# The low parts of all weight tiles: from VectorE to a program on GpSimd

## The chip, the cores and the metric

The kernel runs on one core of one Trainium2 chip. The core has TensorE (matrix products into PSUM), VectorE and ScalarE (elementwise work), GpSimd (elementwise work on SBUF only) and SyncE, which here only issues transfers. They run side by side and meet at semaphores. The metric is the device time of one execution in microseconds; lower is better.

## The reference, cut to what matters

The input is one sequence of 1024 positions with 1024 features, in float32. It goes through three blocks, in short:

```
# first block
proj = rmsnorm(x, mix_norm_g) @ w_in                      # q, k, v, g, u, sv
ret = silu(g) * rmsnorm(retention_chunkwise(rotary(q), rotary(k), v))
sgu = spatial_gating_chunked(gelu(u), gelu(sv))
x = x + concatenate([ret, sgu]) @ w_out
a, b = split(causal_depthwise_conv(rmsnorm(x, ffn_norm_g) @ w_up))   # width 3
x = rmsnorm(x + (silu(a) * b) @ w_down, final_norm_g)                # 2816 wide
# second block
glu_a, glu_b, z_conv, q, k, v, z_att = split(rms_norm(x) @ w_in + b_in)
y_conv = conformer_conv(glu_a, glu_b)         # glu_a * sigmoid(glu_b), 31 taps,
                                              # layer norm, silu, @ pw_w
y_att = neighbourhood_attention(q, k, v, rpb) # 8x16 windows of a 16x64 grid
y = concatenate([grouped_rms_norm(y_conv) * silu(z_conv),
                 grouped_rms_norm(y_att) * silu(z_att)])
x = rms_norm(x + y @ w_out, final_g)
# third block
h = layer_norm(x)
mix = concatenate([rms_norm(stick_breaking_attention(q, k, v)),
                   rms_norm(sliding_window_attention(q, k, v))]) @ w_out   # from h @ w_in
h = layer_norm(ALPHA * h + mix)
gate, up = split(h @ w_gate_up)
return layer_norm(ALPHA * h + (silu(gate) * up) @ w_down)            # 2816 wide
```

Each block has norms over the features before and after its parts. Nearly all of the arithmetic is in the products `h @ w` of the activations with the weight matrices, and these have to be as exact as a float32 product.

## The kernel before, in words

The activations lie transposed, with features on the 128 partitions and the 1024 positions along the row. The residual `x` stays in SBUF for the whole kernel.

**Weight stream.** All weights are packed into one stream of 228 tiles of 128x1024 float32 (512 KB each). A tile is what one output of 128 features needs from all 1024 inputs, or a part of an MLP down projection, or half of the pointwise product. For a product that is close to float32, each weight is split into two float32r numbers: w_hi, a rounded copy, and w_lo = w_raw - w_hi. The activations are split in the same way into h_hi and h_lo. Each product is then three matmuls, `w_hi h_hi + w_lo h_hi + w_hi h_lo`, in `gemm` (line 407) or, where two tiles run together behind a norm, in `project_pair` (line 437). A tile is 48 matmuls of 128x512.

**Who does what for tile t.** Each of w_raw, w_hi and w_lo has two buffers, used by tiles of even and odd number.
- SyncE loads w_raw (line 2109) once w_lo of tile t-2 has been made.
- ScalarE copies w_raw into w_hi (line 866) once the load has landed and TensorE is through with tile t-2.
- VectorE subtracts (line 1436) once w_hi of tile t is there.
- TensorE takes tile t once w_lo of tile t is there.

**Order.** Each engine's program is one Python class that writes its instructions in the order in which the engine runs them; there is no planner. `split_up_to(t)` in `ScalarProgram` and in `VectorProgram` puts the splits of all tiles up to t, as far as they haven't been issued, at the place of the call. So on both engines a split stands in a queue with the norms, taps, softmax steps and residual sums around it, and what is behind a split waits for what the split waits for. `Queue.wait_ge` leaves out a wait that the engine has passed before.

**Places that come up below.**
- A pair of tiles follows each norm or each mixer: tiles 0, 24, 32, 98, 128, 136, 154 and 162 and the ones after them.
- First MLP (tiles 32 to 97): per group of six tiles, up projections `a` and `b` with three taps each on ScalarE and VectorE, their product `mlp_tp`, its parts `mlp_act_hi` and `mlp_act_lo` (line 1686), and two down tiles whose eight sums VectorE adds to the residual (line 1680). At its end, VectorE also sums squares (line 1600).
- Conformer (tiles 98 to 109): for each of four channel tiles VectorE forms conv_u (line 1721) and runs 24 taps (28 for the last) over it, alternately into y and conv_part (line 1734); TensorE runs the other taps (line 628) and then a mean over the four tiles (line 448).
- `y_low` (line 1457 through `low`), `rotary` (lines 1511 to 1515), the last steps of neighbourhood attention (lines 1834 and 1838), and the sum for the layer norm's mean (line 2040).
- GpSimd has one instruction of the program, a memset (line 2150) whose result SyncE waits for at the start.

## Time and profile before

| | |
|---|---|
| time, median of 3 runs | 3603.32 us (3598.68 to 3607.8) |
| the profiled execution | 3605.6 us, of which the span from first to last instruction is 3604.3 us |
| mean granted TensorE clock in it | 0.969 |
| TensorE busy | 3386.6 us, 94% |
| VectorE busy | 1570.9 us, 44% |
| ScalarE busy | 1121.3 us, 31% |
| GpSimd busy | 0.4 us |

Busy time is the time in which an engine has an instruction in flight, as a share of the span. A matmul's end is modelled, and matmuls overlap, so one of 400 ns starts every 234 ns. An idle time is put down to the instruction whose semaphore came last.

### The profile page before, as it was taken

Reading aid. Unit: us, or ns where it says so; the run is one execution under the profiler, and the core shown is the slowest. Engines: PE = TensorE matmul, PEld = TensorE weight load, DVE = VectorE, ACT = ScalarE, POOL = GpSimd, SP = SyncE. Lnnn points to the kernel's source line nnn. Section 1 sums busy time; section 2 is a strip of 40 time slices with the busy share of each in tenths; the row PEclk is TensorE's granted clock in tenths of the full one; section 3 lists DMA queues with packets and bytes.
Section 4 is the critical chain, followed back from the end, with each engine's and each line's share of the span. In section 5 each row is a group of like instructions: output and inputs, shape, how many; then the busy total and the mean of one; then the engine's idle time right before and its main releaser. Section 6 shows DMA issues by size and latency. Waiting matters only on the chain. (4 is left out here: it accounts for less than half of the span.)

```text
span 3604.3 us, 33001 instructions
## 1 busy us (share of the span) xinstructions
PE 3386.6 (94%) x13906; PEld 2495.8 (69%) x13906; DVE 1570.9 (44%) x2227; ACT 1121.3 (31%) x1603; POOL 0.4 (0%) x5
## 2 busy tenths in 40 slices
PE   8999899999999899899999899999869999999997
PEld 5887678888888667566667545546347688888885
DVE  4432354444445589433334532342573432332334
ACT  3223332222122331544442532342561411111113
POOL 0000000000000000000000000000000000000000
PEclk9999999999999999999999999998999999999998
DMA  3211111111111101101001000000001111111111
GB/s 128 75 54 38 32 40 48 52 41 53 47 47 47 41 28 31 35 24 30 24 24 41 30 12 24 18 6 18 7 18 41 30 53 47 47 47 47 47 47 53
DMA packets 48818, 141.76 MB, mean 39 GB/s; under 512 B 12790, under 2 KB 16670, under 8 KB 48542
## 3 DMA queue, kind: packets, MB, share of 16 engines
q1 hardware_dynamic: 48670, 139.65, 12.7%
q8 instruction: 110, 1.80, 0.2%
q14 instruction: 38, 0.31, 0.0%
HBM read 135.36 MB, written 9.77 MB: 40 GB/s over the span
## 5 line engine op out<-in xcount | busy, mean ns | idle before, releaser
L407 PE MATMUL psum<-h_hi,w_hi 128*128 128x512 f32 x2656 | 846.9, 400 | 9.9 <-DVE w_lo L1436 3.1
L407 PE MATMUL psum<-h_lo,w_hi 128*128 128x512 f32 x2656 | 838.5, 397 | 0.0
L407 PE MATMUL psum<-h_hi,w_lo 128*128 128x512 f32 x2656 | 838.5, 397 | 0.0
L407 PEld LDWEIGHTS psum<-h_hi,w_hi 128*128 128x128 f32 x2656 | 499.0, 189 | 141.8 <-issue 19.9
L407 PEld LDWEIGHTS psum<-h_lo,w_hi 128*128 128x128 f32 x2656 | 501.1, 189 | 122.0
L407 PEld LDWEIGHTS psum<-h_hi,w_lo 128*128 128x128 f32 x2656 | 500.9, 189 | 122.2
L1436 DVE TENSOR_TENSOR w_lo<-w_raw,w_hi 128x1024 fp32r<-128x1024 f32 x228 | 278.6, 1222 | 619.1 <-ACT w_hi L866 619.0
L866 ACT ACTIVATE w_hi<-w_raw 128x1024 fp32r<-128x1024 f32 x228 | 239.4, 1050 | 457.5 <-PE psum L407 386.8
L1680 DVE TENSOR_TENSOR residual<-residual,psum 128x1024 f32<-128x1024 f32 x176 | 214.6, 1219 | 170.4 <-PE psum L407 169.3
L407 PE MATMUL psum<-mlp_act_hi,w_hi 128*128 128x512 f32 x704 | 219.8, 394 | 12.8 <-DVE mlp_act_lo L1686 11.3
L407 PE MATMUL psum<-mlp_act_hi,w_lo 128*128 128x512 f32 x704 | 218.6, 392 | 0.0
L407 PE MATMUL psum<-mlp_act_lo,w_hi 128*128 128x512 f32 x704 | 218.5, 392 | 0.0
L407 PEld LDWEIGHTS psum<-mlp_act_hi,w_hi 128*128 128x128 f32 x704 | 133.5, 190 | 42.3 <-DVE mlp_act_lo L1686 12.2
L407 PEld LDWEIGHTS psum<-mlp_act_hi,w_lo 128*128 128x128 f32 x704 | 133.5, 190 | 28.2
L407 PEld LDWEIGHTS psum<-mlp_act_lo,w_hi 128*128 128x128 f32 x704 | 133.3, 189 | 27.9
L1079 ACT ACTIVATE mlp_act_hi<-mlp_tp 128x1024 fp32r<-128x1024 f32 x44 | 46.6, 1060 | 321.5 <-DVE mlp_tp L2058 233.1
L1629 DVE SCALAR_TENSOR_TENSOR mlp_tb<-psum,vectors,mlp_tb 128x1023 f32<-128x1023 f32 (+1 forms) x44 | 56.4, 1282 | 162.8 <-ACT mlp_tb L1019 162.0
L437 PE MATMUL psum<-h_hi,w_hi 128*128 128x512 f32 x256 | 88.0, 427 | 34.7 <-ACT h_hi L919 15.3
L1892 DVE TENSOR_SCALAR sb_mag<-psum 128x512 f32<-128x512 f32 (+3 forms) x96 | 52.9, 557 | 147.1 <-PE psum L754 147.0
L2058 DVE TENSOR_TENSOR mlp_tp<-mlp_ta,psum 128x1024 f32<-128x1024 f32 x22 | 26.9, 1221 | 180.1 <-PE psum L407 178.3
L763 PE MATMUL psum<-sb_soft,common 128*128 128x512 f32 (+3 forms) x192 | 98.1, 597 | 5.3 <-DVE sb_soft L1908 5.3
L754 PE MATMUL psum<-sb_q,sb_k 64*128 64x512 f32 (+3 forms) x192 | 94.7, 602 | 4.9 <-ACT sb_vtok L1294 4.9
(272 smaller groups left out, 3419.1 us busy)
## 6 DMA issues: line engine op xcount, KB each, us to landing
w_raw<-in_weights SPq DMA_DIRECT2D x228, 512.0 KB, 3.6
residual<-in_x_t SPq DMA_DIRECT2D x8, 512.0 KB, 8.6
out_t<-residual SPq DMA_DIRECT2D x8, 512.0 KB, 3.0
rel_copies<-rel_rows SPq DMA_DIRECT2D x8, 480.0 KB, 6.3
na_bias<-rel_copies SPq DMA_DIRECT2D x8, 240.0 KB, 4.2
band_copies<-band_rows SPq DMA_DIRECT2D x8, 192.0 KB, 6.2
ret_rotary<-in_rotary SPq DMA_DIRECT2D x1, 1024.0 KB, 8.2
swa_bias<-band_copies SPq DMA_DIRECT2D x4, 256.0 KB, 2.7
```

The costliest lines, as they stand in the source:

```text
L407: ins = self.pe.matmul(out[:, s], w[:, k, at:at + P], src(k, low)[:, s], start=(k == 0 and part == 0), stop=(k == n_k - 1 and part == 2))
L437: ins = pe.matmul(out[j][:, s], w[:, k, :], self.h(k, low)[:, s], start=(k == 0 and part == 0), stop=(k == KD - 1 and part == 2))
L754: pe.matmul(z[:, c0:HALF], m.sk[hp, kb * CH:(kb + 1) * CH], m.sq[hp, qh * HALF + c0:(qh + 1) * HALF], start=True, stop=False, skip_group_c ...
L763: ins = pe.matmul(z[:, c0:HALF], m.c("neg_tri"), m.soft[:, i % 3, c0:HALF], start=False, stop=False, skip_group_check=True)
L866: self.act.activation(self.m.w_hi[:, n % 2, :], self.m.raw[:, n % 2, :], ACT.Copy).then_inc(*self.to("w_hi", n))
L1079: self.act.activation(m.act_hi[:, c % 2, :], m.tp[:], ACT.Copy).then_inc(*self.to("act_hid_hi" + name, c))
L1436: self.dve.tensor_tensor(self.m.w_lo[:, n % 2, :], self.m.raw[:, n % 2, :], self.m.w_hi[:, n % 2, :].bitcast(F32), ALU.subtract).then_inc( ...
L1629: dve.scalar_tensor_tensor(y[:, back:S], m.place["proj", t][:, 0:S - back], w, y[:, back:S], ALU.mult, ALU.add).then_inc(*to("dve_tap_" + ...
L1680: self.dve.tensor_tensor(x, x, self.m.place["down", t, n], ALU.add).then_inc(*self.to("dve_down", t, n))
L1892: dve.tensor_scalar(m.mag[:, i % 4, c], m.place["pe_sz", p, i][:, c], LN_TOP, None, ALU.min).then_inc(*to("dve_slow", p, i))
L2058: dve.tensor_tensor(m.tp[:], m.ta[:], m.place["proj", b[c]], ALU.mult).then_inc(*to("dve_mmlp3", c))
```

## The change

All calls of `VectorProgram.split_up_to` go, and with them the method. A new program for GpSimd holds the subtractions of all 228 tiles in a row, each behind its wait for w_hi. It begins with the memset that stood in the code of SyncE's program. In the MLP of the third block the wait for `mlp_act_hi` of the product before becomes a wait for its `mlp_act_lo`.

```diff
-    def split_up_to(self, t):
-
-        while self.next_split <= min(t, N_TILES - 1):
-            n = self.next_split
-            self.q.wait_ge(*self.on("w_hi", n))
-            self.dve.tensor_tensor(self.m.w_lo[:, n % 2, :], self.m.raw[:, n % 2, :], self.m.w_hi[:, n % 2, :].bitcast(F32),
-                                   ALU.subtract).then_inc(*self.to("w_lo", n))
-            self.next_split += 1
...
         for i in range(CONV_TILES - 1):
             t = B2 + 2 + 2 * i
-            self.split_up_to(t + 1)
             taps(i, 0, TAPS // 4)
-            self.split_up_to(t + 2)
             taps(i, TAPS // 4, TAPS - PE_TAPS)
             total(i, TAPS - PE_TAPS)
             gated(i + 1)
...
             q.wait_ge(*on("proj", b[c]))
             if c:
-                q.wait_ge(*on("act_hid_himlp3", c - 1))
+                self.after("dve_hid_lomlp3", c - 1)
             dve.tensor_tensor(m.tp[:], m.ta[:], m.place["proj", b[c]], ALU.mult).then_inc(*to("dve_mmlp3", c))
...
+class PoolProgram:
+
+
+    def __init__(self, nc, mem, s):
+        self.q, self.pool, self.m, self.on, self.to = Queue(nc.gpsimd), nc.gpsimd, mem, s.on, s.to
+
+    def program(self):
+        m = self.m
+        self.pool.memset(m.y[0:NA_HEADS * REL_H, KD - 1, 0:REL_PAD], 0.0).then_inc(*self.to("pool_padded"))
+        for n in range(N_TILES):
+            self.q.wait_ge(*self.on("w_hi", n))
+            self.pool.tensor_tensor(m.w_lo[:, n % 2, :], m.raw[:, n % 2, :], m.w_hi[:, n % 2, :].bitcast(F32),
+                                    ALU.subtract).then_inc(*self.to("w_lo", n))
...
-        self.nc.gpsimd.memset(padded, 0.0).then_inc(*self.to("pool_padded"))
         q.wait_ge(*on("pool_padded"))
...
         VectorProgram(nc, mem, s).program()
+        PoolProgram(nc, mem, s).program()
         SyncProgram(nc, mem, s, tensors).program()
```

## Rows read from the trace of the kernel before

**Rows 1.** the page, busy time, share and instructions of each engine.
```profile
PE 3386.6 (94%) x13906; PEld 2495.8 (69%) x13906; DVE 1570.9 (44%) x2227; ACT 1121.3 (31%) x1603; POOL 0.4 (0%) x5
```

**Rows 2.** the page, costliest groups: xcount | busy us, mean ns | idle before.
```profile
L1436 DVE TENSOR_TENSOR w_lo<-w_raw,w_hi 128x1024 fp32r<-128x1024 f32 x228 | 278.6, 1222 | 619.1 <-ACT w_hi L866 619.0
```

**Rows 3.** TensorE's waits: us in total, times, longest.
```profile
PE psum L437 <- DVE w_lo L1436: 9.4, 2, 5.7
```

**Rows 4.** timeline (start us, us), tile 26, behind a pair.
```profile
417.48 1.06 ACT L866 ACTIVATE w_hi<-w_raw 128x1024 fp32r<-128x1024 f32 x1 [14.83 <-PE psum L437]
421.44 0.63 PE L407 MATMUL psum<-h_hi,w_hi 128*128 128x512 f32 x2
```

**Rows 5.** timeline, first MLP, tile 41.
```profile
598.05 1.04 ACT L866 ACTIVATE w_hi<-w_raw 128x1024 fp32r<-128x1024 f32 x1
598.18 1.22 DVE L1686 TENSOR_TENSOR mlp_act_lo<-mlp_tp,mlp_act_hi 128x1024 fp32r<-128x1024 f32 x1 [1.13 <-ACT mlp_act_hi L1079]
602.93 0.63 PE L407 MATMUL psum<-h_hi,w_hi 128*128 128x512 f32 x2
```

**Rows 6.** groups of instructions on GpSimd.
```profile
L2150 POOL MEMSET y<- 120x128 f32 x1 | 0.2, 205 | 0.3 <-POOLq L2310 0.3
L2310 POOL MEMSET const-float32-0.0<- 128x1 f32 x1 | 0.1, 100 | 0.2 <-issue 0.2
```

**Rows 7.** timeline, tile 113.
```profile
1518.64 1.06 ACT L866 ACTIVATE w_hi<-w_raw 128x1024 fp32r<-128x1024 f32 x1 [4.82 <-DVE na_q L1806]
1521.08 0.74 PE L407 MATMUL psum<-h_hi,w_hi 128*128 128x512 f32 x2 [3.11 <-DVE w_lo L1436]
```

**Rows 8.** timeline, start of the kernel.
```profile
24.30 2.36 DVE L1436 TENSOR_TENSOR w_lo<-w_raw,w_hi 128x1024 fp32r<-128x1024 f32 x2 [24.30 <-ACT w_hi L866]
27.80 0.75 DVE L1451 SCALAR_TENSOR_TENSOR norm_buf<-residual,vectors,norm_rstd 128x512 f32<-128x512 f32 x1 [1.15 <-ACT norm_rstd L877]
58.49 0.70 PE L407 MATMUL psum<-h_hi,w_hi 128*128 128x512 f32 x2 [1.34 <-DVE ret_q L1513]
```

**Rows 9.** conformer: stretch, length, busy PE PEld DVE ACT POOL, clock, DMA; then timeline.
```profile
1305.00:1339.00 34.00, 34.00 (x123) 23.00 (x122) 33.90 (x30) 6.17 (x11) 0.00 (x0) 1.00 0.11 31
1338.27 1.22 DVE L1721 TENSOR_TENSOR conv_u<-conv_ga,conv_gb 128x1024 f32<-128x1024 f32 x1
1371.89 1.22 DVE L1721 TENSOR_TENSOR conv_u<-conv_ga,conv_gb 128x1024 f32<-128x1024 f32 x1
1445.33 1.22 DVE L1743 TENSOR_TENSOR y<-y,psum 128x1024 f32<-128x1024 f32 x1
1339.54 0.70 PE L628 MATMUL psum<-conv_u,conv_diags 128*128 128x512 f32 x1
1374.15 0.59 PE L628 MATMUL psum<-conv_u,conv_diags 128*128 128x512 f32 x1
1449.91 7.03 PE L448 MATMUL psum<-y,common 128*128 128x512 f32 x16
```

**Rows 10.** timeline, end of the first MLP, tile 98.
```profile
1237.00 1.04 ACT L866 ACTIVATE w_hi<-w_raw 128x1024 fp32r<-128x1024 f32 x1
1238.27 2.35 DVE L1600 TENSOR_TENSOR norm_acc<-norm_acc,norm_buf 128x1024 f32<-128x1024 f32 x2
1240.54 1.22 DVE L1436 TENSOR_TENSOR w_lo<-w_raw,w_hi 128x1024 fp32r<-128x1024 f32 x1
1254.33 3.75 PE L614 MATMUL psum<-norm_acc,common 128*128 128x512 f32 x4 [4.97 <-DVE norm_acc L1600]
```

**Rows 11.** timeline, before the second mixer's output, tile 129.
```profile
1895.90 1.04 ACT L866 ACTIVATE w_hi<-w_raw 128x1024 fp32r<-128x1024 f32 x1
1897.34 1.23 DVE L1838 TENSOR_TENSOR y<-na_t,na_gate 128x1024 f32<-128x1024 f32 x1
```

**Rows 12.** timeline, before the third block's second layer norm, tile 163.
```profile
2795.37 1.06 ACT L866 ACTIVATE w_hi<-w_raw 128x1024 fp32r<-128x1024 f32 x1 [10.18 <-PE psum L407]
2796.57 1.23 DVE L2040 TENSOR_TENSOR norm_acc<-norm_acc,residual 128x1024 f32<-128x1024 f32 x1
```

More of the change, by code:

```diff
@@ L1462, in program @@
         m = self.m
-        self.split_up_to(1)
         self.split_norm("n1", (m.n_buf0, m.n_buf1), m.n_rstd, lambda k: m.v("mix_norm_g", k), "act_n1_rstd")
@@ L1495, in y_low @@
     def y_low(self, block, ahead):
-        self.split_up_to(ahead)
         for k in range(KD):
@@ L1519, in retention @@
         mask, qdec, cdec = m.table[:, 0:P], m.table[:, P:2 * P], m.table[:, 2 * P + 1:2 * P + 2]
-        self.split_up_to(2)
         q.wait_ge(*on("rotary_loaded"))
@@ L1553, in retention @@
                 ins.then_inc(*(to("dve_rchain", h, n) if n < NCH - 1 else to("dve_rstate", h)))
-            self.split_up_to(t + 3)
             if h < RET_HEADS - 1:
@@ L1558, in retention @@
             dve.tensor_scalar(m.y[:, h, :], m.place["pe_ro", h], m.v("ret_norm_g", h), None, ALU.mult).then_inc(*to("dve_ro", h))
-            self.split_up_to(t + 4)
             if h < RET_HEADS - 1:
@@ L1576, in gating @@
             dve.tensor_tensor(m.rk[:], m.rk[:], m.place["pe_smean", g], ALU.subtract).then_inc(*to("dve_scent", g))
-            if g < SGU_GROUPS - 1:
-                self.split_up_to(t + 1)
             q.wait_ge(*on("act_srstd", g, 1))
@@ L1583, in gating @@
             dve.tensor_tensor(w_t, w_t, m.c("tril_t"), ALU.mult).then_inc(*to("dve_swm", g))
-            if g < SGU_GROUPS - 1:
-                self.split_up_to(t + 2)
             q.wait_ge(*on("pe_smix", g))
@@ L1642, in up @@
             self.hidden("mlp1", c)
-        self.split_up_to(MLP1 + 2)
         taps_a(0)
         up(0)
-        self.split_up_to(MLP1 + 3)
         taps_a(1)
-        self.split_up_to(MLP1 + 4)
         up(1)
@@ L1652, in mlp1 @@
             c = 2 * g
-            self.split_up_to(a[c] + 1)
             for half in range(2):
                 t = d[2 * g - 2 + half]
-                self.split_up_to(t + 1)
                 for n in range(4):
@@ L1660, in mlp1 @@
                         tap(m.ta, "a", a[c], c, c, 1 + n)
-            self.split_up_to(b[c] + 1)
             up(c)
-            self.split_up_to(a[c + 1] + 1)
             taps_a(c + 1)
-            self.split_up_to(b[c + 1] + 1)
             up(c + 1)
@@ L1668, in mlp1 @@
             t = d[2 * NGROUP - 2 + half]
-            self.split_up_to(t + 1)
             for n in range(4):
@@ L1707, in norm4 @@
         dve.tensor_tensor(m.gains[:], m.vec[:, g3:g3 + KD], m.vec[:, g4:g4 + KD], ALU.mult).then_inc(*to("dve_gains"))
-        self.split_up_to(B2 + 1)
         self.combine("n4", "act_n3_rstd", ("pe_n4_mean",))
@@ L1746, in conformer @@
         dve.memset(m.u[:, PAD + S:], 0.0)
-        self.split_up_to(B2 + 2)
         gated(0)
@@ L1753, in conformer @@
             t = B2 + 2 + 2 * i
-            self.split_up_to(t + 1)
             taps(i, 0, TAPS // 4)
-            self.split_up_to(t + 2)
             taps(i, TAPS // 4, TAPS - PE_TAPS)
@@ L1761, in conformer @@
         for j in range(CONV_TILES):
-            self.split_up_to(B2 + 8 + j + 1)
             taps(i, 9 * j, min(9 * j + 9, n))
@@ L1794, in pointwise @@
         for n in range(4):
-            if n % 2 == 0:
-                self.split_up_to(B2 + 13 + n // 2)
             if n:
@@ L1809, in neighbourhood @@
             t = B2 + 14 + 4 * p
-            self.split_up_to(t + 1)
-            self.split_up_to(t + 2)
             q.wait_ge(*on("na_bias_loaded", p))
@@ L1814, in neighbourhood @@
                               ALU.add).then_inc(*to("dve_nmask", p))
-            self.split_up_to(t + 3)
-            self.split_up_to(t + 4)
             self.after("dve_nmask", p)
@@ L1855, in after_mix2 @@
             ins.then_inc(*to("dve_l1_acc", n))
-        self.split_up_to(B3 + 1)
         q.wait_ge(*on("pe_l1_mean", 1))
@@ L1880, in stick_breaking @@
         dve, q, m, on, to = self.dve, self.q, self.m, self.on, self.to
-        self.split_up_to(B3 + 2)
         dve.tensor_copy(m.ident_b[:], m.c("ident"))
@@ L1884, in stick_breaking @@
         for p in range(4):
-            self.split_up_to(B3 + 2 + 4 * p + 4)
             q.wait_ge(*on("pe_svtok", p))
@@ L1946, in add_squares @@
             dve.tensor_tensor(m.total[:, s], m.total[:, s], m.y[:, p, s], ALU.add).then_inc(*to("dve_wtotal", p, half))
-        self.split_up_to(B3 + 19)
         q.wait_ge(*on("sinks_loaded"))
@@ L2077, in mlp3 @@
             t = d[2 * NGROUP - 2 + half]
-            self.split_up_to(t + 1)
             for n in range(4):
```

18 lines of the change are left out of this document (removed).

## The prediction, written before the changed kernel was run

> **What bounds the kernel now.** I read the page's totals first: TensorE is busy for 3386.6 us of the 3604.3 us span, VectorE for 1570.9, GpSimd for 0.4 [rows 1]. The table of costliest groups then says where VectorE's time goes: the moved instruction, line 1436, is its largest group, 228 times 1222 ns, 278.6 us [rows 2]. It would be easy to call that a gain of 278 us. So the third view is TensorE's list of waits, and there w_lo stands with 9.4 us in two waits on line 437 and one 3.1 us wait on line 407 [rows 3, 7]. The rest of TensorE's idle time (3604.3 - 3386.6 = 218 us in all) belongs to norms, softmax loops and activation chains. The weight split is a side stream: the kernel ends when TensorE has gone through its 228 tiles, and VectorE matters only where TensorE waits for it.
>
> **What must stay true for the stream to be hidden.** ScalarE makes w_hi of tile t once tile t-2 is finished, then w_lo follows, and tile t starts when TensorE has done tile t-1. I compared the end of w_hi with the first matmul for all tiles. Three kinds matter.
> - Most tiles have 5 to 12 us there.
> - In the first MLP two tiles of each group of six have less. Tile 41: w_hi ends at 598.05 + 1.04 = 599.09, its first matmul starts at 602.93, so 3.84 us; VectorE is in a product with two SBUF inputs until 599.40, which leaves 3.53 us behind that [rows 5]. There are 20 such tiles, and tile 35, with 3.3.
> - The tile behind a pair (26, 100, 130, 156, 164) has 421.44 - 418.54 = 2.90 us [rows 4].
> - Tile 113 has none to spare: w_hi ends at 1519.70 and TensorE starts at 1521.08 after a 3.11 us wait; the 1.38 us between them are the subtraction and its hand-overs [rows 7].
>
> **What one subtraction costs on GpSimd (D).** The trace has no such instruction. The only rows are memsets: 120x128 in 205 ns, 128x1 in 100 ns [rows 6]. The slope is 105 / 127 = 0.83 ns a column. A subtraction has two streams in and one out. If all three overlapped, D = 0.10 + 1024 x 0.83 ns = 0.95 us, the lower end. If each cost a whole memset, eight times the 205 ns row, D = 3 x 1.64 = 4.9 us, the upper end. One after another at the slope: 0.10 + 3 x 0.85 = 2.6 us. I take 2.4, near that, since some overlap is likely. The Trainium skill, "GPSIMD Engine Reference", section 3.1, gives 4497 ns for a float32 tensor_tensor of 2048 columns; half is 2.25 us, an estimate of mine from that page, and by it the sum below would be about 1 us smaller.
>
> **The changes, part by part, without contention between the two engines.**
> - 228 subtractions leave VectorE. Hidden by TensorE everywhere but at these places. Tile 2's stands ahead of the first rotary; TensorE waits 1.34 us for that rotary at 58.49 [rows 8], and the 1.23 us go: -1.2. Tile 98's, at 1240.54, stands in a stretch where VectorE is back to back up to the norm sum that TensorE awaits for 4.97 us [rows 10]: -1.1. Tile 129's holds up TensorE by its last 0.1 us only: h_hi, made from the y product that ends at 1898.57, takes another 1.1 us [rows 11], and is needed too: -0.1.
> - The conformer is where VectorE is full: 33.90 busy of 34.00 us [rows 9]. It is not the bound there: TensorE is busy 34.00 of 34.00. Its taps of channel tile 1 start at 1339.54, 0.05 us behind the conv_u product (1338.27 + 1.22), so the subtractions taken off VectorE there, ten of 1.13 us (what one adds back to back: two such instructions last 2.35 us [rows 10]), buy 0.1.
> - 228 subtractions come to GpSimd, which does nothing else: 228 x 2.4 = 547 us in a span of 3604. Tile 113: D replaces 1.22, TensorE starts +1.2 later. Tiles behind pairs: 2.4 < 2.90, hidden. MLP tiles: hidden. The cover ends at D = 2.9 for five tiles and at 3.8 for 21.
> - The padded memset is issued from the new program as its first instruction, as now: 0. In the last MLP, product c now waits for VectorE's own low part c-1, which ended many us before, while line 2058 waits for a projection anyway: 0. No DMA is added or moved; a load waits for w_lo of two tiles before, and has around 11 us over its 3.6.
> Sum: -1.2 - 1.1 - 0.1 - 0.1 + 1.2 = -1.3 us.
>
> **With contention.** Every VectorE instruction at these places that I use below has two SBUF inputs, as has the subtraction on GpSimd; today all of that runs on one engine, so no row shows them side by side. The bound from below is no interference (the sum above). From above: GpSimd keeps VectorE out for the whole of D. I take the upper end, as a mechanism of this kernel: both engines pull two float32 streams from the same partitions at the same moment. The Trainium skill, "SBUF — State Buffer", section "Who interferes with whom", states just this rule: a VectorE instruction with two SBUF inputs and a GpSimd one that reads SBUF exclude each other, and the second waits in full. No row here shows it; by it the sum is the one that follows, without it the one above.
> - Conformer. Taps are scalar_tensor_tensor with conv_u and an accumulator, back to back. Up to conv_u of channel tile 1, three subtractions (tiles 101 to 103) would hold VectorE for 3 x 2.4 = 7.2 while two of 1.13 are gone: +4.9. The next round has two of each: +4.8 - 2.3 = +2.5, sum 7.4; but that conv_u ends at 1373.11 and TensorE's taps start at 1374.15, 1.04 of slack [rows 9]. TensorE: +6.4. The end adds nothing: VectorE would be 10 x (2.4 - 1.13) = 12.7 late, from 1446.55 to 1459.3, and the last four of the sixteen mean matmuls, 5.2 us into the row of 1449.91, would be at 1461.5.
> - Tile 98: w_hi is done at 1238.04, norm_acc starts 1238.27 [rows 10]. GpSimd is first, VectorE loses 2.4 and has saved 1.13: +1.2 in place of -1.1.
> - Tile 129: w_hi done 1896.94; either the y product of 1897.34 goes first and w_lo ends at 1901.0 (+1.2), or GpSimd does and y is 2.4 late [rows 11]. Taken: +1.8.
> - Tile 163: w_hi done 2796.43, norm_acc on the way to the layer norm's mean starts 2796.57 [rows 12]: 0 or +2.4, taken +1.2.
> - Start: the subtractions of tiles 0 and 1 would last from 24.3 to 29.1; the first scaling at 27.80 slips [rows 8]: by 1.3, of which some 0.5 falls into the wait that its second half has anyway: +0.8.
> - Unchanged: tile 2 -1.2, tile 113 +1.2.
> Sum: 6.4 + 1.2 + 1.8 + 1.2 + 0.8 - 1.2 + 1.2 = +11.4 us. The profiled execution took 3605.6 (span 3604.3 and 1.3 around it), 2.3 above the median of 3603.3; so 3617.0 in its terms, and 3614.7 for the median. I give **3614 us**.
>
> **Rivals.**
> - No contention: the first sum, 3603.3 - 1.3 = **3602**. For it: nothing in the trace shows interference, all of it is assumed. This is the case on the other side, faster than before, by tile 98 and the rotary; it decides if VectorE's taps take what they take now beside a GpSimd instruction. Even then it is far less than 0.3%. To reach 0.3% TensorE would have to lose 11 us of waits of which w_lo and what stands behind it hold at most 12.5 + 2.4.
> - GpSimd is slow, D = 4.9: w_lo becomes late on its own. 21 tiles x (4.9 - 3.6) = 27, five pairs x 2.0 = 10, tile 113 3.7, and in the conformer (3 x 4.9 - 2.3) + (9.8 - 2.3) - 1.0 = 19 with contention. About +45 without, +65 with it: **3650 to 3670**. Against it: it needs twice my D; float32r output is the one thing that the memset rows can't speak for.
> - VectorE keeps GpSimd out: back-to-back taps leave no opening until the one-SBUF-input sum with psum at the end of each channel tile. That is at about 1337, while two tiles of 11.5 us stand before the taps of 1339.54, so the first of them is due at 1316: TensorE would stand some 20 us in each of three rounds, **3660**. Against: a waiting instruction would have to be passed over some twenty times.
> - The subtraction isn't moved at all (a low part still on VectorE): the diff takes out every call, so I give it nothing.
>
> **How the numbers follow.** Contention at about D = 2.4: 0.55. Its own range, D from 2.0 to 3.0 and with half to all of D lost, is 3607 to 3622. No contention: 0.28. Slow GpSimd: 0.09. VectorE keeping GpSimd out: 0.08. The range 3600 to 3635 leaves out the centres of the last two, 0.17 of the chance, and little else. A measurement of this kernel tells about 0.3% (11 us, so 3592.5 and 3614.1) from no change. The likeliest case lies at that border: half of it is slower, half the same. Slower: 0.27 + 0.09 + 0.08 = 0.44. Same: 0.28 + 0.25 = 0.53. Faster: 0.03.
>
> **What would show it.** In the profile after: about 228 GpSimd subtractions with D read off directly; VectorE's total down by 279 us if nothing interferes, but its tap rows longer than now, or gaps between them, if it does. TensorE's list of waits should have conv_u at 1340 and 1375 with some 5 us and 1.5 us, and no rotary at 58. The time from w_hi to the first matmul of tile 113 gives D plus the hand-over. I am wrong in the mechanism if the taps are untouched, and wrong in size if D is over 3 us or if w_lo turns up in TensorE's waits in the MLPs.

## The result, and the profile after

| | before | after |
|---|---|---|
| time, us: median (lowest to highest), runs beside each other | 3604.2 (3598.7 to 3607.8), 4 | 3635.9 (3628.9 to 3641.5), 4 |
| ratio, 95% interval | 1 | 1.0092 (1.0078 to 1.0105) |
| profiled execution, time and span | 3605.6, 3604.3 | 3641.5, 3640.1 |
| VectorE busy | 1570.9 | 1374.3 |
| TensorE busy, mean granted clock | 3386.6, 0.969 | 3402.8, 0.962 |

The kernel is 31.6 us slower by the medians. My forecast was 3614 and my range ended at 3635.

The group of the moved instruction in the changed kernel's page, and TensorE's waits (us in total, times, longest):

```profile
L2043 POOL TENSOR_TENSOR w_lo<-w_raw,w_hi 128x1024 fp32r<-128x1024 f32 x228 | 589.8, 2587 | 2986.5 <-ACT w_hi L866 2986.5
```
```profile
PE psum L437 <- ACT h_hi L927: 11.4, 2, 7.7
PE psum L407 <- POOL w_lo L2043: 15.6, 2, 11.4
PE psum L628 <- DVE conv_u L1686: 5.0, 1, 5.0
PE psum L454 <- DVE norm_acc L1984: 4.7, 1, 4.7
PE psum L454 <- DVE norm_acc L1806: 0.8, 1, 0.8
```

Three things are to be seen. VectorE lost 228 instructions that took 278.6 us [rows 2], but only 196.6 us of busy time: 82 us came back, in instructions that last longer than before. The mean of a subtraction on GpSimd is 2587 ns, and 198 of the 228 last less than 2.5 us (the shortest 2.34); two last 9.7 and 27.0 and lift the mean. And w_lo still stands in TensorE's waits: not with the 9.4 us of [rows 3], but with one wait of 11.4 us that was not there.

That wait is in the conformer. The timeline of the changed kernel there, GpSimd first, then VectorE, then TensorE (start us, us):

```profile
1330.52 9.67 POOL L2043 TENSOR_TENSOR w_lo<-w_raw,w_hi 128x1024 fp32r<-128x1024 f32 x1 [21.48 <-ACT w_hi L866]
1340.82 2.66 POOL L2043 TENSOR_TENSOR w_lo<-w_raw,w_hi 128x1024 fp32r<-128x1024 f32 x1 [0.63 <-ACT w_hi L866]
...
1419.31 30.33 POOL L2043 TENSOR_TENSOR w_lo<-w_raw,w_hi 128x1024 fp32r<-128x1024 f32 x2 [8.88 <-ACT w_hi L866]
```
```profile
1336.67 1.28 DVE L1699 SCALAR_TENSOR_TENSOR conv_part<-conv_u,vectors,conv_part 128x1024 f32<-128x1024 f32 x1
1337.98 3.29 DVE L1705 TENSOR_TENSOR y<-y,conv_part 128x1024 f32<-128x1024 f32 x1
...
1342.44 2.12 DVE L1686 TENSOR_TENSOR conv_u<-conv_ga,conv_gb 128x1024 f32<-128x1024 f32 x1
...
1442.84 1.28 DVE L1699 SCALAR_TENSOR_TENSOR conv_part<-conv_u,vectors,conv_part 128x1024 f32<-128x1024 f32 x1
1444.15 3.25 DVE L1705 TENSOR_TENSOR y<-y,conv_part 128x1024 f32<-128x1024 f32 x1
```
```profile
1344.61 2.07 PE L628 MATMUL psum<-conv_u,conv_diags 128*128 128x512 f32 x2 [5.03 <-DVE conv_u L1686]
...
1446.37 1.22 PE L407 MATMUL psum<-h_hi,w_hi 128*128 128x512 f32 x2 [11.36 <-POOL w_lo L2043]
```

The subtraction of tile 103 starts at 1330.52, and the taps of VectorE go on at 1.28 us each, untouched. Only the sum at 1337.98, which comes 0.03 us behind the end of the last tap because it waits for that tap's own result, is 3.29 us long in place of 1.22, and 2.2 us into it GpSimd is done. So GpSimd did nothing for 7.5 us and then all its work behind the first opening. Tile 108 (the first of the two in the 30.33 us row, up to 1446.32) is the same over 20 boundaries between taps: asked at 1419.31, through at 1444.15, and TensorE had wanted the tile since 1435.0.

The second thing is TensorE's clock. "Granted clock" is the share of full speed: 1.00 is 2.4 GHz, 0.50 is 1.2 GHz, and a value between them means that the stretch holds both. Stretches of the changed kernel behind these waits and behind two layer norms (length, busy PE PEld DVE ACT POOL, granted clock, DMA):

```profile
1342.00:1352.00 10.00, 7.39 (x12) 3.31 (x13) 9.96 (x10) 1.11 (x1) 1.48 (x1) 0.66 0.27 89
1446.00:1456.00 10.00, 9.63 (x31) 7.70 (x32) 2.62 (x2) 0.00 (x0) 3.64 (x2) 0.71 0.36 107
2022.00:2035.00 13.00, 9.69 (x12) 3.36 (x11) 9.12 (x8) 5.50 (x7) 0.71 (x1) 0.50 0.13 40
2827.00:2841.00 14.00, 9.05 (x11) 3.38 (x12) 10.13 (x8) 3.17 (x3) 1.32 (x1) 0.51 0.12 37
```

In the kernel before, the same four places had 1.00, 1.00, 0.87 and 0.88. At the second layer norm of the third block TensorE waits 4.71 us for a sum in place of 2.57, and is granted 1.2 GHz for 13.7 us in a row where the kernel before had 3.4 us of it. How much of this comes from the longer wait is taken up behind experiment 12.

To place the whole loss I took the time from the first matmul of one tile to that of another, in every trace (us; the last line is after minus before):

```
tiles         0-2   98-100  100-103 103-107 107-110 110-116 116-130 130-136 136-154 154-164 164-227
before       27.5    23.9    57.7    64.5    57.9   133.3   317.4    99.3   681.1   141.0   707.8
after        24.9    25.2    65.0    64.5    70.2   135.4   320.4   103.7   681.4   147.0   706.4
difference   -2.6    +1.4    +7.3     0.0   +12.4    +2.1    +3.0    +4.3    +0.2    +6.0    -1.4
```

With +1.0 at the start, +0.4 in tiles 2 to 97 and +1.7 behind tile 227 these are the 35.8 us between the two spans. 19.7 of them are in the conformer (tiles 100 to 110), some 15 at four places where a norm or a product is due (tiles 113, 129, 137, 163).

### The profile page after: what moved, and what is told of

Its sections match the earlier page's. It is cut to its first block and busy times, and to the rows that moved or that the text cites. A ratio compares the mean times of both kernels' runs of the same rounds, so it can differ in the third digit from the quotient of the medians.

```text
span 3640.1 us, 33002 instructions
## 1 busy us (share of the span) xinstructions
PE 3402.8 (93%) x13906; PEld 2504.8 (69%) x13906; DVE 1374.3 (38%) x1999; ACT 1121.5 (31%) x1603; POOL 590.2 (16%) x233
## 5 line engine op out<-in xcount | busy, mean ns | idle before, releaser
L2043 POOL TENSOR_TENSOR w_lo<-w_raw,w_hi 128x1024 fp32r<-128x1024 f32 x228 | 589.8, 2587 | 2986.5 <-ACT w_hi L866 2986.5
```

Of the source, the lines that this page charges most:

```text
L2043: self.pool.tensor_tensor(m.w_lo[:, n % 2, :], m.raw[:, n % 2, :], m.w_hi[:, n % 2, :].bitcast(F32), ALU.subtract).then_inc(*self.to("w_lo ...
```

## The experiments

Each kernel ran beside the kernel before on its chip, whose medians there were 3600.3 to 3600.8 us. All kernels that split the subtractions between the two engines have this in VectorE's loop, and the set ON_POOL differs:

```diff
+            self.next_split += 1
+            if n in ON_POOL:
+                continue
             self.q.wait_ge(*self.on("w_hi", n))
```

**1. The conformer's ten subtractions back on VectorE.**
```diff
+ON_POOL = set(range(N_TILES)) - set(range(101, 111))
```


> The changed kernel with the ten subtractions of tiles 101 to 110 (conformer) back on VectorE at their old places, all others on GpSimd. Theory (VectorE's back-to-back two-input taps and GpSimd exclude each other, and in the conformer GpSimd can be kept out until VectorE itself waits): TensorE gets back the 5.0 us wait on conv_u, the 11.4 us wait on w_lo of tile 108 and the slow clock behind both; by the difference of the two traces, tile by tile, 7.3 + 11.5 + 2.6 - 1.7 = 19.7 us less than the changed kernel: about 3616, 12 above the kernel before. Rival (GpSimd slows VectorE a little everywhere, and the conformer has no special part; then ten subtractions of 228 carry 4% of the loss): 3634 to 3636.

Measured: 3620.1 us (3618.2 to 3624.7), ratio 1.0051 (1.0034 to 1.0068), so 19 above the kernel before. By the trace the conformer's part is gone, to the last tenth: tiles 100 to 110 take 178.4 us, where before has 180.1 and after 199.8. The rival falls. I had put too little outside the conformer: the other places hold more than 12 us (15 by the traces, 19 by the medians).

**2. Only these ten on GpSimd.**
```diff
+ON_POOL = set(range(101, 111))
```


> The kernel before with only the subtractions of tiles 101 to 110 on GpSimd. Theory: it loses in the conformer what the changed kernel lost there, 5.0 us at conv_u of channel tile 1, 11.4 at tile 108 if GpSimd is locked out again, and the slow clock behind: 3604 + 20 = 3624; if a lock-out is a matter of which moment GpSimd asks in, single executions scatter between +8 (no lock-out) and +20 or more. Rival (loss spread over all tiles): 3604 to 3607.

Measured: 3629.5 us, ratio 1.0082 (1.0052 to 1.0112); the four executions took 3622.2, 3626.4, 3632.6 and 3640.9. By the medians ten instructions of 228 bring most of the loss (ratio 1.0082 of 1.0092), and with them the executions scatter over 19 us. But this ratio and that of experiment 1 (1.0051) add up to more than the whole, so it overstates the ten's share: in the profiled execution tiles 100 to 110 take 193.4 us, 13.3 more than before, and the rest of the 20.4 us between the two spans lies where nothing was changed (3.6 at tiles 154 to 164, 2.9 at 138 to 154, and smaller ones). In the one profiled (3626.4) GpSimd's rows are:

```profile
1330.38 9.70 POOL L2113 TENSOR_TENSOR w_lo<-w_raw,w_hi 128x1024 fp32r<-128x1024 f32 x1 [21.46 <-ACT w_hi L871]
...
1436.27 17.60 POOL L2113 TENSOR_TENSOR w_lo<-w_raw,w_hi 128x1024 fp32r<-128x1024 f32 x2 [15.32 <-ACT w_hi L871]
```

Tile 103 is kept out for 9.7 us as in the changed kernel; tile 108 gets in at once this time (2.57 us), and tile 109 is kept out for 14.3 (the first of the two in the second row).

**3. VectorE stops for GpSimd.**
```diff
+            self.after("w_lo", t + 1)
             taps(i, 0, TAPS // 4)
+            self.after("w_lo", t + 2)
             taps(i, TAPS // 4, TAPS - PE_TAPS)
...
+            self.after("w_lo", B2 + 8 + j + 1)
             taps(i, 9 * j, min(9 * j + 9, n))
```


> The changed kernel, but VectorE waits for GpSimd's low part at the places in the conformer where it used to make that low part itself (before tap 0 and 7 of channel tiles 0 to 2, before taps 0, 9, 18, 27 of the last). Nothing is moved back; VectorE only stops there until GpSimd is done. Theory (GpSimd is kept out by VectorE's unbroken row of taps): no GpSimd subtraction of 10 or 27 us is left, tile 108 has its low part before it is due, the 11.4 us wait and the slow clock behind it go: 12 to 14 us less than the changed kernel, about 3622 to 3624; the 5 us wait on conv_u stays. Rival (tile 108 was late because GpSimd is slow beside taps, not because it was kept out; then an additional wait of VectorE can only cost): 3636 or more, and single subtractions of over 5 us stay.

Measured: 3623.6 us (3623.2 to 3627.9), ratio 1.0061 (1.0045 to 1.0078) against 1.0092 for the changed kernel: ten waits more, 11 us less. GpSimd and VectorE around tile 108:

```profile
1418.88 4.50 POOL L2046 TENSOR_TENSOR w_lo<-w_raw,w_hi 128x1024 fp32r<-128x1024 f32 x1 [8.73 <-ACT w_hi L866]
```
```profile
1419.90 1.28 DVE L1699 SCALAR_TENSOR_TENSOR y<-conv_u,vectors,y 128x1024 f32<-128x1024 f32 x1
1423.42 1.29 DVE L1699 SCALAR_TENSOR_TENSOR conv_part<-conv_u,vectors,conv_part 128x1024 f32<-128x1024 f32 x1 [2.24 <-POOL w_lo L2046]
```

The subtraction was passed over at one boundary (1419.90), VectorE stopped at 1421.18, and 2.2 us after that it was done. Tiles 107 to 110 take 56.2 us (70.2 in the changed kernel); the 7.3 us at tile 103 stay, as expected. A stop of VectorE lets a waiting GpSimd in. That the subtraction would have stayed out for the rest of the row without it is seen in the changed kernel, not in this run. I had also written that no long subtraction would be left; tile 103's is (9.7 us), since its stop comes later than its lock-out.

**4. Taps with one SBUF input.** The accumulation of taps 2 and up is left out.
```diff
-                    ins = dve.scalar_tensor_tensor(out, src, w, out, ALU.mult, ALU.add)
+                    ins = dve.tensor_reduce(out[:, 0:1], src, AX_X, ALU.add)
```


> The changed kernel, in which taps 2 and up of the conformer on VectorE are sums over the row (tensor_reduce: one SBUF input, one column out) in place of scalar_tensor_tensor with two SBUF inputs; it leaves out the accumulation of the depthwise convolution. VectorE stays back to back in them, each reading 1024 columns. Theory (two SBUF inputs are what collides with GpSimd): no GpSimd subtraction that starts within these reductions lasts more than 2.6 us, none of the reductions is put off, the waits on conv_u and on w_lo of tile 108 and the slow clock behind them are gone: about 20 us less than the changed kernel, 3612 to 3617. Rival (any unbroken row of VectorE instructions keeps GpSimd out): the 10 and 27 us subtractions stay, as does the time.

Measured: 3617.2 us, ratio 1.0044 (1.0028 to 1.0061). VectorE and GpSimd at tile 108, and VectorE at tile 104:

```profile
1410.32 1.21 DVE L1699 TENSOR_REDUCE y<-conv_u 128x1 f32<-128x1024 f32 x1
1411.45 1.21 DVE L1699 TENSOR_REDUCE conv_part<-conv_u 128x1 f32<-128x1024 f32 x1
...
1338.42 0.81 DVE L1694 TENSOR_SCALAR y<-conv_u,vectors 128x1024 f32<-128x1024 f32 x1
1339.14 2.85 DVE L1696 TENSOR_SCALAR conv_part<-conv_u,vectors 128x1024 f32<-128x1024 f32 x1
```
```profile
1410.76 2.36 POOL L2043 TENSOR_TENSOR w_lo<-w_raw,w_hi 128x1024 fp32r<-128x1024 f32 x1 [9.70 <-ACT w_hi L866]
...
1339.10 2.35 POOL L2043 TENSOR_TENSOR w_lo<-w_raw,w_hi 128x1024 fp32r<-128x1024 f32 x1 [7.89 <-ACT w_hi L866]
```

Beside the reductions neither engine sees the other, though their row is as unbroken as that of the taps. So it is not VectorE's being busy. The edit changed one thing more: a reduction writes one column and a tap 1024. That the writing is not what collides is seen in the changed kernel, in the sum behind the one that was held up at tile 108. It has one input in SBUF and one in PSUM, writes 1024 columns, and lasts 1.22 us as before although it falls into the second subtraction of the 30.33 us row above:

```profile
1447.44 1.22 DVE L1708 TENSOR_TENSOR y<-y,psum 128x1024 f32<-128x1024 f32 x1
```

The same holds for the 40 residual sums with PSUM that overlap a subtraction in that trace (1.22 us each).

One instruction with a single SBUF input does collide, the tensor_scalar at 1339.14: it takes 0.75 us for 1024 columns when alone (the reductions 1.21) and 2.85 here. A copy in the changed kernel does so too (2.82 in place of 0.69). The Trainium skill, "SBUF — State Buffer", section "Who interferes with whom", has both: a VectorE instruction contends with GpSimd's reads if it has two SBUF inputs or runs in one of the modes that use both ports, and not otherwise. The trace agrees on two inputs against one; that the tensor_scalar and the copy run in such a mode no row says, only that they are the quick ones. Tiles 100 to 110 take 178.9 us.

**5. The lock-out by itself.** All low parts on VectorE; twelve subtractions that nobody needs on GpSimd.
```diff
+        for i in range(CONV_TILES):
+            for j in (3, 8, 16):
+                q.wait_ge(*on("dve_tap", i, j))
+                if cols := next(delays):
+                    self.pool.memset(m.probe[:, 2, 0:cols], 0.0)...
+                self.pool.tensor_tensor(m.probe[:, 2, :], m.probe[:, 0, :], m.probe[:, 1, :], ALU.subtract)...
```


> The kernel before, all low parts on VectorE, with twelve subtractions of the same size that nobody needs on GpSimd beside the taps, each asked for when a certain tap has ended and delayed by 0 to 1.1 us (a memset of 0 to 960 columns in between). It measures the lock-out by itself. Theory: some of the twelve take 2.4 us and delay a tap by 2.4, others do not start until VectorE waits at the end of its channel tile, up to 20 us later, and which of the two depends on the moment within the running tap at which they ask (in the changed kernel those that asked 0.75 to 0.99 us into a tap came through, those at 0.39 and 1.03 did not); the memsets in between, with no SBUF input, last what their size says and hold up nobody. Rival (no lock-out, GpSimd always gets its turn at the next boundary between two taps): all twelve last 2.4 to 3.7 us.

The ninth and the tenth of GpSimd's pairs:

```profile
1412.68 0.80 POOL L2114 MEMSET probe<- 128x832 f32 x1 [8.38 <-DVE y L1735]
1413.56 9.64 POOL L2116 TENSOR_TENSOR probe<-probe 128x1024 f32<-128x1024 f32 x1
1431.70 0.90 POOL L2114 MEMSET probe<- 128x960 f32 x1 [8.50 <-DVE conv_part L1735]
1432.68 3.53 POOL L2116 TENSOR_TENSOR probe<-probe 128x1024 f32<-128x1024 f32 x1
```

Nine subtractions got in at the next boundary and last 2.2 us plus the rest of the tap that ran; each made the next tap 3.4 us long in place of 1.28. Two missed one boundary, one lasted 9.6 us. The memsets, which have no SBUF input, last what their size says (0.80 us for 832 columns) and delayed no tap. One of the two that missed a boundary had asked only 0.02 us ahead of it. The one of 9.6 us had asked 1.07 us into a tap, the two of 9.7 us above at 1.01 and 1.03: that looked like a window near the end of a tap.

**6. Sixteen other moments, with stops of VectorE.**
```diff
+                    if (i, j - 5) in DELAYS:
+                        self.after("pool_probed", i, j - 5)
```


> As the kernel with twelve unneeded subtractions on GpSimd beside the taps, with sixteen of them at other moments within a tap (seven at 1.0 to 1.25 us, the rest at 0.2 to 1.0, the last four of these in the last channel tile), and VectorE waits for each before the fifth tap after the one that set it off, so that no lock-out hides the next. Theory (the outcome hangs on the moment within the tap): those at 0.2 to 0.98 us get in at the next boundary and last 2.4 + the rest of the tap; those at 1.0 to 1.17 are kept out for all boundaries up to VectorE's stop, and last 5 us. Rival (it hangs on something else, as which channel tile or buffer): outcomes that differ for the same moment; the last channel tile, where one at 0.39 was kept out, is the place to look.

The theory fell. GpSimd's third and fourth, and the tap put off by the fourth:

```profile
1329.49 0.79 POOL L2116 MEMSET probe<- 128x832 f32 x1 [5.99 <-DVE y L1739]
1330.36 2.46 POOL L2118 TENSOR_TENSOR probe<-probe 128x1024 f32<-128x1024 f32 x1
1338.81 0.82 POOL L2116 MEMSET probe<- 128x864 f32 x1 [5.99 <-DVE y L1739]
1339.71 2.38 POOL L2118 TENSOR_TENSOR probe<-probe 128x1024 f32<-128x1024 f32 x1
```
```profile
1338.61 1.27 DVE L1739 SCALAR_TENSOR_TENSOR conv_part<-conv_u,vectors,conv_part 128x1024 f32<-128x1024 f32 x1
1339.81 3.37 DVE L1739 SCALAR_TENSOR_TENSOR y<-conv_u,vectors,y 128x1024 f32<-128x1024 f32 x1
```

They asked 1.07 and 1.10 us into a tap and got in at the very next boundary, as did all sixteen. The last channel tile behaved like the others.

**7. The same without the stops.** The two lines of 6 are taken out.

> The sixteen unneeded subtractions on GpSimd at the same moments, without the stops of VectorE. With the stops all sixteen came through at the first or second boundary between taps, also those at 1.03 to 1.13 us into a tap, so the moment within the tap does not decide. Theory 1 (chance: most requests come through, some are kept out, stops or not): nearly the same picture, with 0 to 4 kept out for several taps. Theory 2 (a stop a few taps ahead is what lets GpSimd in): about half of the sixteen or more are kept out until VectorE stops at the end of the channel tile.

The same sixteen durations to 0.01 us, none kept out. Theory 1's low end (0 of 16); a stop a few taps ahead is not what lets GpSimd in.

**8. Both lock-outs once more.** The changed kernel and experiment 5, unchanged.

> The changed kernel once more, for the lock-outs alone. Theory 1 (whether GpSimd gets in is fixed by the program): the subtraction of tile 103 lasts 9.7 us again and that of tile 108 27.0. Theory 2 (it changes from one execution to the next with small shifts in time; the executions of the changed kernel lay 12 us apart): tile 103, which took 9.7 us in three kernels, does so again, but 108 or 109 last something else.

> The kernel with twelve unneeded subtractions once more. Theory 1 (fixed by the program): the ninth is kept out for 9.6 us again, the tenth and the twelfth for one tap more than needed, the others for none. Theory 2 (chance from execution to execution): others are kept out, or none.

```profile
1419.54 30.32 POOL L2043 TENSOR_TENSOR w_lo<-w_raw,w_hi 128x1024 fp32r<-128x1024 f32 x2 [8.88 <-ACT w_hi L866]
```
```profile
1412.55 2.47 POOL L2116 TENSOR_TENSOR probe<-probe 128x1024 f32<-128x1024 f32 x1
...
1431.75 8.28 POOL L2116 TENSOR_TENSOR probe<-probe 128x1024 f32<-128x1024 f32 x1
```

In the changed kernel both come again to 0.02 us (9.67 and 27.00; time 3641.6). In the other kernel they don't: the ninth gets in at once, the tenth is kept out and lasts 8.3 us. It missed five boundaries and got in at the sixth, in the middle of VectorE's row, with no stop and no opening there. The tap that it put off, behind a subtraction of VectorE's own:

```profile
1436.55 1.22 DVE L1437 TENSOR_TENSOR w_lo<-w_raw,w_hi 128x1024 fp32r<-128x1024 f32 x1
1437.68 3.43 DVE L1735 SCALAR_TENSOR_TENSOR conv_part<-conv_u,vectors,conv_part 128x1024 f32<-128x1024 f32 x1
```

So neither of my theories holds alone: some places repeat, some change though the moment within the tap moved by less than 10 ns. What decides stays open, and so does whether a lock-out lasts to the end of the row. (The single executions of experiments 5 to 8 with unneeded subtractions took 3622.5 to 3630.1 us.)

**9. Two subtractions of 228.**
```diff
+ON_POOL = {137, 163}
```


> The kernel before with two of its 228 subtractions on GpSimd, those of tiles 137 and 163. They fall beside the last addition of the sums that the layer norms behind the second and third mixer wait for. Theory (each puts that addition off by 2.1 to 2.3 us; TensorE waits 0.8 and 2.1 us longer and then runs at the low granted clock): the two steps seen in all four kernels with these two on GpSimd, 4.3 and 4.3 to 5.4 us, come from them alone: 8 to 10 us more than before, about 3610. Rival (these steps have another cause and the clock drop is not tied to the two): the added waits alone, 0 to 3 us.

Measured: 3607.5 us, ratio 1.0023 (1.0014 to 1.0032): 7 to 8 us for two instructions, the low end of what I gave. The interval begins at 5 us, so they cost more than the 2.1 us that TensorE waits longer. In the profiled execution (3612.5, above the median) the step is at tile 163. VectorE, GpSimd and TensorE there, and the 14 us behind (columns as above):

```profile
2797.18 3.36 DVE L2047 TENSOR_TENSOR norm_acc<-norm_acc,residual 128x1024 f32<-128x1024 f32 x1
```
```profile
2797.11 2.34 POOL L2113 TENSOR_TENSOR w_lo<-w_raw,w_hi 128x1024 fp32r<-128x1024 f32 x1 [795.81 <-ACT w_hi L871]
```
```profile
2800.59 2.93 PE L459 MATMUL psum<-norm_acc,common 128*128 128x512 f32 x3 [4.71 <-DVE norm_acc L2047]
```
```profile
2798.00:2812.00 14.00, 8.92 (x10) 3.36 (x11) 10.13 (x8) 3.17 (x3) 1.45 (x1) 0.52 0.13 37
```

GpSimd was 0.07 us ahead, the addition took 3.36 us in place of 1.23 [rows 12], TensorE waited 2.1 us more and ran at 0.52 of its clock; tiles 154 to 162 take 5.2 us more than in the trace of before. At tile 137 VectorE's addition is held up just the same (3.37 us), but nothing comes of it: tiles 130 to 136 take 99.6 us (99.3 before). TensorE's first matmuls of the norm ran at the low clock in this execution and lasted until the second sum was there.

**10. Tiles 128 to 130 with 137.**
```diff
+ON_POOL = {128, 129, 130, 137}
```


> The kernel before with four subtractions on GpSimd, those of tiles 128, 129, 130 and 137. Tile 137's alone (with 163's) left no step behind the second mixer, while the four kernels that also had 128 to 130 on GpSimd showed 4.3 us there. Theory (the later start of the pair at tile 128, a wait of 7.7 in place of 5.7 us, comes before the wait at the norm, and the two together bring the 13.7 us at half the clock): steps of 1.5 to 2 us at tile 128 and of 4.3 us at tile 136, in all 6 us more than before. Rival (the 4.3 us need other tiles on GpSimd too): the step at 128 alone, 2 us.

Measured: 3616.4 us, ratio 1.0042 (1.0028 to 1.0056). TensorE at the layer norm, and the stretch behind it:

```profile
1998.72 2.40 PE L459 MATMUL psum<-norm_acc,common 128*128 128x512 f32 x4 [3.73 <-DVE norm_acc L1607]
2002.00 2.93 PE L459 MATMUL psum<-norm_acc,common 128*128 128x512 f32 x3 [0.88 <-DVE norm_acc L1861]
```
```profile
2000.00:2015.00 15.00, 11.57 (x16) 4.05 (x15) 11.13 (x9) 5.86 (x8) 0.87 (x1) 0.54 0.12 35
```

The steps are those of the changed kernel: tiles 116 to 130 take 320.0 us (317.4 before), 130 to 136 103.7 (99.3). In the profiled executions the 4.3 us came with the delay at tile 129 ahead of the one at 137, and not without it. The median is 16 us above before, twice the 7 us that these steps add up to; in its profiled execution tiles 138 to 154 took 654.4 us, where that stage took between 644.9 and 657.3 us over all traces whatever the kernel. I can't say how much of the 16 it holds.

**11. Lateness without GpSimd.** The computation is complete; `hold_up` is two multiplications that nobody needs.
```diff
+                if n == KD - 1:
+                    self.hold_up()
                 ins = dve.scalar_tensor_tensor(m.m_acc[:], x, g, m.m_acc[:], ALU.mult, ALU.add)
```
(and the same ahead of the last addition at the third mixer)

> The kernel before, GpSimd doing nothing, with two more VectorE multiplications of 128x1024 that nobody needs ahead of the last addition of the sums that the layer norms behind the second and the third mixer wait for. They put these two sums off by 2.3 us each, as GpSimd's subtraction did in the changed kernel. Theory (a longer wait of TensorE there costs itself plus matmuls at the low granted clock behind it, whoever causes the wait): the wait grows by 0.8 to 2.3 us in each place, TensorE is then granted 0.5 of its clock for 10 us and more, and the two places together cost 8 to 11 us, like the 4.3 and 5.2 us in the changed kernel: about +9. Rival (the slow clock has to do with GpSimd or came by chance, and a wait costs what it lasts): the sum of the longer waits alone, +3.

Measured: 3606.5 us, ratio 1.0010 (1.0000 to 1.0019), between theory and rival, and the interval (0 to 7 us) holds the rival's 3. TensorE at the third mixer, and the stretch behind it:

```profile
2794.93 2.93 PE L454 MATMUL psum<-norm_acc,common 128*128 128x512 f32 x3 [4.84 <-DVE norm_acc L2049]
```
```profile
2792.00:2806.00 14.00, 8.58 (x12) 3.22 (x13) 11.26 (x11) 3.17 (x3) 0.00 (x0) 0.63 0.14 37
```

There it looks like the theory, without GpSimd: 4.84 us of wait in place of 2.57, a clock of 0.63 in place of 0.88, and tiles 154 to 162 take 121.8 us in place of 116.9, of which 2.3 are the wait. But the trace of before is at the low end there, as the numbers behind experiment 12 show. At the second mixer the wait came out as 0.29 us and the step as 0.3, since TensorE's own first sum ran at the low clock just then (3.18 us where the changed kernel's took 2.53) and hid it.

**12. More of it at the second mixer.** Three multiplications there, none at the third.

> The kernel before with three unneeded VectorE multiplications (3.6 us) ahead of the last addition of the layer norm sum behind the second mixer, nothing at the third, and nothing on GpSimd. With two of them the sum was 2.3 us late, yet TensorE showed no wait above 0.3 us there, because its own first sum ran at the low granted clock. Theory (a wait of TensorE there brings the long low-clock stretch with it, whoever makes it): a second wait of 1 to 2 us at this layer norm, 0.5 of the clock for over 10 us as in the changed kernel, and a step of 4 to 6 us in the times of the tiles behind. Rival (the long stretch needs GpSimd): a stretch of 3.4 us as in the kernel before, and a step of 1 to 2 us, the wait itself.

Measured: 3606.6 us, ratio 1.0012 (1.0004 to 1.0021). TensorE at the second mixer:

```profile
1999.70 1.98 PE L454 MATMUL psum<-norm_acc,common 128*128 128x512 f32 x4 [1.32 <-DVE norm_acc L1861]
```
```profile
1995.00:2010.00 15.00, 11.02 (x22) 4.30 (x23) 14.06 (x13) 8.16 (x10) 0.00 (x0) 0.89 0.11 35
```

The wait is there, 1.32 us, but the clock behind it is 0.89, the short stretch of the kernel before, and tiles 130 to 136 took 100.5 us (99.3): the rival's picture, or no step at all, since five traces in which this sum was not put off have 100.8 (experiments 6, 7, 13, 14 and the repeat of 5 in 8). But the profiled execution, 3601.5 us, is the fastest of ten, and eight of the others lie at 3604.6 to 3607.5, 4 to 7 above before, which is the theory's size. The experiment does not decide; where the others lost these microseconds no trace shows.

What the steps at the two mixers are worth shows only against all traces. Ten traces have the 2.57 us wait of before at the third mixer, and tiles 154 to 162 take from 116.8 to 119.8 us in them, 118.4 in the mean; the seven with the longer wait of 4.7 or 4.8 (experiment 11's among them) take 121.5 to 122.3. So the longer wait costs some 3.6 us by the means, and of the 5.2 between the traces of before and after up to 2.9 come without it. The low clock too comes without a longer wait. Experiment 5's trace there:

```profile
2817.37 3.22 PE L455 MATMUL psum<-norm_acc,common 128*128 128x512 f32 x4 [2.57 <-DVE norm_acc L2042]
```
```profile
2818.00:2832.00 14.00, 11.51 (x19) 4.40 (x18) 9.59 (x9) 5.17 (x5) 0.00 (x0) 0.64 0.13 37
```

That is the wait of before with the clock of experiment 11. At the second mixer tiles 130 to 138 take 126.4 to 128.8 us where the sum was not put off, and 130.7 in the changed kernel. At the first channel tile of the conformer there is no such doubt: tiles 100 to 103 take 57.7 us in all eight traces in which GpSimd does nothing there, and 65.0 in the changed kernel.

**13. Everything back that stands beside a norm.**
```diff
+ON_POOL = set(range(N_TILES)) - {0, 1, 98, 99, 100, 113, 128, 129, 130, 137, 163} - set(range(101, 111))
```


> The kernel with the conformer's ten subtractions back on VectorE, and also those of tiles 0, 1, 98 to 100, 113, 128 to 130, 137 and 163, all of which stand beside a norm or a product that TensorE waits for; the 207 others on GpSimd. Theory (the loss outside the conformer sits at these few places): 3597 to 3602, no more than the kernel before, 18 to 20 us less than with the conformer's alone moved back. Rival (the softmax loops of the two attention stages, 111 to 162, lose too beside GpSimd): 5 us or more above before.

Measured: 3597.4 us, ratio 0.9994 (0.9985 to 1.0003). The 207 subtractions left on GpSimd cost nothing, their mean is 2435 ns, and 22.7 us separate this from experiment 1. TensorE's list of waits has none on GpSimd. The softmax loops did not suffer: tiles 138 to 154 took 644.9 us, the least of all traces.

**14. Only the first mixer's and the MLPs' tiles on GpSimd.**
```diff
+ON_POOL = set(range(2, 98)) | set(range(164, 228))
```


> The kernel before with the subtractions of tiles 2 to 97 and 164 to 227 on GpSimd (first mixer, both MLPs), and those of tiles 0, 1 and 98 to 163 (conformer, pointwise, neighbourhood, norms, attention blocks) on VectorE as before. Theory (the whole loss sits where TensorE waits for VectorE or w_lo): nothing is lost, and what the changed kernel gained stays: 1.3 us ahead of the first rotary and about 1.3 more in the mixer and at tile 34: 2 to 3 us less than before. Rival (GpSimd's 160 subtractions disturb VectorE everywhere, which shows in time): at least 5 us more than before.

Measured: 3597.7 us, ratio 0.9992 (0.9983 to 1.0001). Both versions lie 3 us under the kernel before, and both intervals just include no change. Of the 278.6 us [rows 2] that one hoped to take off VectorE this is what there was to gain.

## Why the prediction was wrong, by its own steps

- **D = 2.4 us: right.** The median of the 228 is 2.40 us. The page figure I had weighed ("GPSIMD Engine Reference", section 3.1, in the Trainium skill) gave 2.25 by my halving; the measurement decides.
- **Tiles behind pairs and in the MLPs hidden: right.** Tiles 164 to 227 take 706.4 us in the changed kernel and 706.3 in that of experiment 2, where VectorE makes their low parts.
- **Contention, by its upper end: right, and shown** by experiments 4 and 9. A VectorE instruction with two SBUF inputs and GpSimd's subtraction exclude each other, and the second waits in full: 1.23 becomes 3.36.
- **conv_u of channel tile 1, +4.9: right as a wait** (5.03 against none), though partly by luck: I had three subtractions holding VectorE for 2.4 each, 7.2 in all, and the trace has three holding it for 2.1 and that of tile 104, which I had left out, for 0.9. Short as a price: the step is 7.3 us, since the clock fell to half for 6.8 us behind it. **The next round, +1.5: none.** Tiles 103 to 107 take 64.5 us in both; TensorE had itself fallen 2.3 us further behind, which with the slack of 1.04 is more than the 2.5 (this is argued, no run tests it).
- **The start, tile 2, tile 113: right.** The rotary's wait [rows 8] is gone; tile 113's wait went from 3.11 [rows 7] to 4.21, +1.1 for my +1.2, and the two tiles behind it lost another 1.0. Tile 98's +1.2 was +0.4 as a step, and TensorE's wait there even fell from 4.97 [rows 10] to 4.0.
- **Tile 129, +1.8: right as a wait** (7.69 against 5.68), 3.0 as a step with tile 130. **Tile 163, +1.2: mis-sized.** I had halved between 0 and 2.4 as if a coin fell. The rows of before held the answer [rows 12]: w_hi ends at 2796.43 and the addition starts at 2796.57, so GpSimd, 0.08 us behind w_hi, is always first. TensorE waited 2.1 longer; the step was 5.2, some 3.6 of it the wait's by all traces.
- **Tile 137: missing from the sum.** It has the same pattern as 163, behind the second mixer. 4.3 us in the changed kernel, at least 1.9 by all traces, and none where tile 137 was moved without tiles 128 to 130 (experiments 9 and 10).
- **The lock-out: in the wrong place.** I had it as a rival with 0.08, priced at 20 us in each of three rounds, against it that GpSimd would have to be passed over some twenty times. It was, at one tile. It came beside plain contention, not in its place, and hit one due tile of ten: 12.4 us. The step that failed is this one: the lock-out was an alternative of 0.08 and stood at nothing in the sum. The next is the price of a wait. Taken together, with the tile left out: 12.4 us at tiles 107 to 110, 4.3 at tile 137, and 2.4, 1.2 and 4.8 more than I gave at tiles 103, 129 and 163 with what follows them, 25.1 together. The other differences cancel to -0.7, and that makes the 24.4 by which 35.8 lies above 11.4.
- **What a wait costs.** I priced each TensorE wait at its own length. In the 10 to 14 us behind them the granted clock was 0.50 to 0.71. At tile 103 5.0 us of wait cost 7.3. At the third mixer 2.1 us cost some 3.6, and by the medians of experiment 9 at least 5. That the wait brings the low clock with it is not shown: experiment 5's trace has the low clock without the longer wait, and experiments 11 and 12 do not decide.
- **The slow-GpSimd rival** was added up wrongly: its terms without contention, 27 + 10 + 3.7, are 41 us and not 45. Nothing hangs on it.

I had also treated contention and lock-out as alternatives, each with its own time, where both held at once.

## What to carry to other kernels

An engine that helps out may hold up the one that it helps: look which instructions of VectorE have two SBUF inputs (or are quick copies and scalings, as the two of experiment 4) and stand just ahead of something that TensorE waits for, and leave GpSimd's SBUF reads out of those few places; here 21 of 228 instructions carried the whole loss, and the other 207 moved at no cost. A row of such VectorE instructions without a stop can keep a GpSimd instruction out for many of them (20 here), so put a stop of VectorE ahead of the moment at which the result is due, or leave it on VectorE. A wait of TensorE can cost more than its length (7.3 us for 5.0 at tile 103): look at the clock that was granted behind it, and compare several traces, since the low clock also moves about by itself.

## What the runs showed that I had not expected

- GpSimd was passed over at 20 boundaries in a row between taps, and was through within 2.2 us of the first opening of 0.03 us. Of the 28 unneeded subtractions of experiments 5 and 6, 25 got in at the next boundary, two missed one, one was kept out for 9.6 us; a repeat of the sixteen without stops changed nothing, a repeat of the twelve changed which were kept out. The moment alone does not decide (1.07 us into a tap: once kept out, three times through).
- A memset on GpSimd beside two-input taps delays nobody and is not delayed: 0.80 us for 832 columns.
- Two instructions on GpSimd made the kernel 7 us slower; the one at tile 163 was 0.07 us ahead of VectorE's.
- Kernels that are alike in a stage differ in it from trace to trace: tiles 98 to 100 took 23.9 or 25.3 us, tiles 138 to 154 from 644.9 to 657.3, tiles 154 to 162 from 116.8 to 119.8. A step of under 3 us in one trace proves nothing in such a stage.
